# Half of projection tile 0 between modulation tiles 2 and 3, and the first norm in two halves of channels

## The chip, the cores and the metric

The kernel runs on one core of a Trainium2 chip as one launch. The metric is device time in microseconds (us), lower is better. TensorE (PE), VectorE (DVE), ScalarE (ACT), GpSimd (POOL) and SyncE (SP) run their own instruction streams side by side and meet at semaphores. Loads and stores are DMA transfers; nearly all of them are issued by SP, in one queue.

## The reference

One decoder step with one layer (DEPTH = 1), for a prompt of 256 tokens and 8 sequences of 8 sample tokens, together 320 tokens of 1024 channels. What lies around the change:

```python
def _layer(x, c, pos, attend, retain, g_mix, g_ffn, w_ada, b_ada, w_in, ...):
    mod = (jnp.einsum('bd,de->be', jax.nn.silu(c), w_ada) + b_ada)[:, None, :]
    sh1, sc1, gt1, sh2, sc2, gt2 = jnp.split(mod, 6, axis=-1)
    h = _rmsnorm(x, g_mix) * (1.0 + sc1) + sh1
    z = jnp.einsum('bsd,de->bse', h, w_in)
    ...   # rotary, sparse attention, retention, merge, output projection: x
    h2 = _rmsnorm(x, g_ffn) * (1.0 + sc2) + sh2
    x = x + gt2 * _moe(h2, ...)        # top-4 of 32 experts
    return x, (k, v, ik, r_state)
```

The modulation `c` is one row for the prompt and one for each of the 8 sample sequences: 9 rows. All arithmetic is float32.

## The kernel before

**Stages.** First come the statistics of x and the first modulation (sc1 and sh1). Then z is projected in 13 column tiles (`ZT`), with indexer, attention and retention work placed between the tiles. Then come the branch merge and the output projection, the second norm and the router, and at last a loop over 32 experts whose weights (12 MB each) stream through a ring of six chunks. The expert loop asks for a chunk when the chunk before it in that place was used (`chunk_used`).

**The head.** x lies transposed in `actT` (called `hT`: 8 chunks of 128 channels, 320 tokens). ACT squares it (L613), PE sums the squares over channels with a matrix of ones (L871, PSUM bank 4), DVE scales the variance (L1586), ACT takes the root (L615), and DVE refines it (L1588 to L1592) and multiplies all of `hT` by it in one instruction (L1593).

**Modulation tiles.** Four tiles of `w_ada`, 512 columns and 2 MB each, are numbered 0 to 3: scale and shift of channels 0 to 511 (tiles 0, 1), scale and shift of channels 512 to 1023 (tiles 2, 3). For each, PE makes eight products of the nine rows with a weight chunk into 32 partitions (L887, 32x512) and adds one to `tile_done`; ACT copies the bank to `partA` (L618, `part_done`); PE turns the nine rows into columns with four products of nine columns each (`modulation_columns`, L878, `tab_done`); DVE adds the bias and, for a scale tile, the norm gain (L1570, L1572). When both tiles of a half are there, DVE's `modulated(half)` (L1578, L1581 four times, L1583) scales and shifts four chunks of `hT` and raises `h_done`. Tile i lies in PSUM bank i. On PE tile i+1 stands before the columns of tile i.

**Projection tile 0.** `prompt_steps` (L921, L922) makes two products of 128 tokens by up to 512 columns at each of the eight chunks, into banks 0 and 1; `sample_steps` (L934, L935) makes two products of 64 tokens by half of the columns, into bank 2. Steps 0 to 3 need `h_done` 1, steps 4 to 7 `h_done` 2.

**Order.** Everything is written out by hand: each engine executes its stream in program order. SP issues cT, pages, x, constants, columns, then the four `w_ada` tiles, then projection tile 0 (`wz[0]`, 2 MB, in a place of its own), then `wz[1]` after the second modulation tile is done (it takes that tile's place) and `wz[2]`, then the indexer's cached keys (32 of 32 KB), then `wz[3]` once `sample_steps(1)` is done. The buffers before:

```python
beside = [z[:, 5448:9544], ring[:, S0 + 10820:S0 + 14916], ring[:, S0 + 5332:S0 + 9428]]
wm = wt + [x.rearrange("p (k n) -> p k n", k=KT) for x in beside[0:2]]
```

`beside[2]` is the home of `wz[0]`.

Of the kernel before, what the change touches and what calls it, by code (L numbers as in the profile page):

```python
# [16 lines left out]
ALU = mybir.AluOpType  # L17
ACT = mybir.ActivationFunctionType
AX = mybir.AxisListType

P = 128
D = 1024
KT = D // P
SEQ = 256
DB, DS = 8, 8
# [8 lines left out]
NTOK = SEQ + NS  # L34
BANK = 512
# [109 lines left out]
def kern(nc, a):  # L145
    with ExitStack() as ctx:
# [24 lines left out]
        def bank(b, n=1):  # L171
            return ps[:, b * BANK:(b + n) * BANK]
# [3 lines left out]
        hT = actT[:, :].rearrange("p (k n) -> p k n", k=KT)  # L176
        cT3 = cT[:, :].rearrange("p (k n) -> p k n", k=KT)
# [3 lines left out]
        wm = wt + [x.rearrange("p (k n) -> p k n", k=KT) for x in beside[0:2]]  # L181
# [4 lines left out]
        partA = scr(0, 2048)  # L186
        sqT = scr(2048, KT * NTOK).rearrange("p (k n) -> p k n", k=KT)
        var_t, root_t, err_t = scr(4608, NTOK), scr(4928, NTOK), scr(10500, NTOK)
        a1T, sh1T = (mods[:, 72 * i:72 * i + 72].rearrange("p (k c) -> p k c", k=KT) for i in range(2))
        badaT, gmixT = cols[:, 0:6 * KT], cols[:, 6 * KT:7 * KT]  # L190
        junk = scr(9500, 256)
        ident = const("ident")
# [87 lines left out]
        w_here = [sem("w_here0"), sem("w_here1")]  # L280
# [3 lines left out]
        tile_done = sem("tile_done")  # L284
        part_done, tab_done = sem("part_done"), sem("tab_done")
# [24 lines left out]
        st_out, side_here = [sem("st_out0"), sem("st_out1")], [sem(f"side_here{i}") for i in range(3)]  # L310
# [29 lines left out]
        def in_tile(name, s):  # L340

            return a[name][s].rearrange("p (k n) -> p k n", k=KT)
# [10 lines left out]
        def _(sp):  # L353
# [4 lines left out]
            sp.dma_start(cst[:, :], a["const"]).then_inc(g_here, 16)  # L358
            sp.dma_start(cols[:, :], a["cols"]).then_inc(g_here, 16)
            sp.dma_start(prow[:, :], a["page_rows"]).then_inc(pr_here, 16)  # L360
            for i in range(4):
                s = (2, 0, 3, 1)[i]
                sp.dma_start(wm[i], in_tile("w_ada", s)).then_inc(w_here[i] if i < 2 else side_here[i - 2], 16)

            def load_z_tiles(first, last):
                for i in range(first, last):
                    c0, w = ZT[i]
                    if i:
                        sp.wait_ge(tile_done, i + 3 if i >= 3 else 3 - i)
                    sp.dma_start(wz[i], a["w_in"][:, KT * c0:KT * (c0 + w)].rearrange("p (k n) -> p k n", k=KT)).then_inc(w_here[i % 2] if i else side_here[2], 16)  # L370

            def load_tile(n, src, dst=None):

# [16 lines left out]
                        sp.dma_start(ikT[b // 2][64 * j:64 * j + 64, n * PAGE:(n + 1) * PAGE],  # L390
                                     a["cache_ikT"][bass.ds(page, 1)].rearrange("a d s -> (a d) s")).then_inc(keys_here[b // 2], 16)

            load_z_tiles(0, 3)
            sp.wait_ge(pr_here, 32)
            load_index_keys(0, 4)
            load_z_tiles(3, 4)
# [211 lines left out]
        def _(act):  # L608
# [6 lines left out]
            nc.scalar.activation(root_t, var_t, ACT.Sqrt).then_inc(rstd_done, 1)  # L615
            for i in range(4):
                act.wait_ge(tile_done, i + 1)
                nc.scalar.activation(partA[:, i * BANK:(i + 1) * BANK], bank(i), ACT.Copy).then_inc(part_done, 1)  # L618

            gate = [ACT.Copy] * 7 + [ACT.Silu] * 2 + [ACT.Sigmoid] * 4  # L620

# [242 lines left out]
        def _(pe):  # L864
# [4 lines left out]
            for k in range(KT):  # L869
                pe.wait_ge(ss_done, 1 + k // 4)  # L870
                last = nc.tensor.matmul(bank(4)[:, 0:NTOK], const("ones"), sqT[:, k, :], start=k == 0, stop=k == KT - 1)  # L871
            last.then_inc(sq_sum, 1)

            def modulation_columns(i):

                pe.wait_ge(part_done, i + 1)
                for c in range(4):
                    last = nc.tensor.matmul(bank(i)[:, (1 + DB) * c:(1 + DB) * (c + 1)],  # L878
                                            partA[:, i * BANK + c * P:i * BANK + (c + 1) * P], const("selT"),
                                            start=True, stop=True)  # L880
                last.then_inc(tab_done, 1)

            for i in range(4):
                pe.wait_ge(w_here[i] if i < 2 else side_here[i - 2], 16)
                for k in range(KT):
                    g = k % 4
                    last = nc.tensor.matmul(bank(i)[32 * g:32 * g + 32, :], cT3[:, k, :], wm[i][:, k, :],  # L887
                                            start=k < 4, stop=k >= 4)
                last.then_inc(tile_done, 1)
                if i:  # L890
                    modulation_columns(i - 1)
            modulation_columns(3)

            def project(wtile, b, w, x=hT, kt=KT, done=tile_done):

# [12 lines left out]
            def prompt_steps(i, k0, k1):  # L908

                w = ZT[i][1]  # L910
                if k0 == 0:
                    if i:
                        pe.wait_ge(*tile_here(i + 4))
                        pe.wait_ge(zp_out, i)
                    else:
                        pe.wait_ge(side_here[2], 16)
                for k in range(k0, k1):
                    if i == 0 and k % 4 == 0:
                        pe.wait_ge(h_done, 1 + k // 4)
                    se = dict(start=k == 0, stop=k == KT - 1)  # L920
                    nc.tensor.matmul(bank(0)[:, 0:w], hT[:, k, 0:P], wz[i][:, k, 0:w], **se)  # L921
                    last = nc.tensor.matmul(bank(1)[:, 0:w], hT[:, k, P:2 * P], wz[i][:, k, 0:w], **se)  # L922
                if k1 == KT:
                    last.then_inc(zp_done, 1)

            def sample_steps(i):

                w = ZT[i][1]
                h = w // 2
                if i:  # L930
                    pe.wait_ge(z_done, i)
                for k in range(KT):
                    se = dict(start=k == 0, stop=k == KT - 1)
                    nc.tensor.matmul(bank(2)[0:NS, 0:h], hT[:, k, 2 * P:NTOK], wz[i][:, k, 0:h], **se)  # L934
                    last = nc.tensor.matmul(bank(2)[NS:P, 0:h], hT[:, k, 2 * P:NTOK], wz[i][:, k, h:w], **se)  # L935
                last.then_inc(tile_done, 1)

            def key_and_index_query_transposes():

# [65 lines left out]
                    nc.tensor.matmul(bank(5 + k)[0:NS], sel, rel_s[:, k * BANK:(k + 1) * BANK], **se)  # L1005
                nc.tensor.matmul(bank(7)[0:NS, NS:NS + DS], sel, rel_s[:, PAST:KEYS], **se).then_inc(ssel_done, 1)

            for i in range(2):
                prompt_steps(i, 0, KT)
                sample_steps(i)  # L1010
            prompt_steps(2, 0, 4)
            key_and_index_query_transposes()
            prompt_steps(2, 4, KT)
# [21 lines left out]
            for t in range(3):  # L1035
                n = TOK[t]
                last = nc.tensor.transpose(bank(6)[:, t * P:t * P + n], z3[0:n, t, CK:CV], ident[0:n, 0:n])
# [144 lines left out]
            for t in range(3):  # L1182
                n = TOK[t]
                for i in range(2):
# [5 lines left out]
                    for k in range(4):  # L1190
                        last = nc.tensor.transpose(bank(b)[:, at + k * n:at + (k + 1) * n],
                                                   h2[0:n, t, (4 * i + k) * P:(4 * i + k + 1) * P], ident[0:n, 0:n])
# [138 lines left out]
            for i in range(6):  # L1331
# [3 lines left out]
                for k in range(2):  # L1335
                    last = nc.tensor.matmul(bank((0, 6)[i % 2] + k)[0:n, :], sel, partB[2 * (i // 2) + k], start=True, stop=True)  # L1336
# [13 lines left out]
            for t in range(3):  # L1350
                n = TOK[t]
                for k in range(KT):
                    last = nc.tensor.matmul(bank(5)[0:n, t * NE:(t + 1) * NE], hT[:, k, t * P:t * P + n], wr[:, k, :],  # L1353
                                            start=k == 0, stop=k == KT - 1)
# [170 lines left out]
        def _(dve):  # L1525
            steps = [0]

            def step(ins):

                steps[0] += 1  # L1530
                ins.then_inc(dve_step, 1)
                dve.wait_ge(dve_step, steps[0])
# [29 lines left out]
            def modulation_columns(i):  # L1562

                half = i // 2
                chunks = slice(4 * half, 4 * half + 4)
                dst = (a1T, sh1T)[i % 2][:, chunks, :]
                src = bank(i)[:, 0:4 * (1 + DB)].rearrange("p (k c) -> p k c", k=4)
                at = KT * (1 - i % 2) + 4 * half
                dve.wait_ge(tab_done, i + 1)
                step(nc.vector.tensor_tensor(dst, src, badaT[:, at:at + 4].unsqueeze(2).broadcast_to([P, 4, 1 + DB]), ALU.add))  # L1570
                if i % 2 == 0:
                    step(nc.vector.tensor_tensor(dst, dst, gmixT[:, chunks].unsqueeze(2).broadcast_to([P, 4, 1 + DB]), ALU.mult))  # L1572

            def modulated(half):

                s = hT[:, 4 * half:4 * half + 4, SEQ:NTOK].rearrange("p k (b t) -> p k b t", t=DS)
                a_s, sh_s = (m[:, 4 * half:4 * half + 4, 1:1 + DB].unsqueeze(3).broadcast_to([P, 4, DB, DS]) for m in (a1T, sh1T))
                nc.vector.tensor_tensor(s, s, a_s, ALU.mult).then_inc(dve_step, 1)  # L1578
                steps[0] += 1
                for k in range(4 * half, 4 * half + 4):  # L1580
                    last = nc.vector.tensor_scalar(hT[:, k, 0:SEQ], hT[:, k, 0:SEQ], a1T[:, k, 0:1], sh1T[:, k, 0:1], ALU.mult, ALU.add)  # L1581
                dve.wait_ge(dve_step, steps[0])
                nc.vector.tensor_tensor(s, s, sh_s, ALU.add).then_inc(h_done, 1)  # L1583
# [6 lines left out]
            step(nc.vector.tensor_tensor(err_t, err_t, var_t, ALU.mult))  # L1590
            step(nc.vector.tensor_scalar(err_t, err_t, -0.5, 1.5, ALU.mult, ALU.add))
            step(nc.vector.tensor_tensor(root_t, root_t, err_t, ALU.mult))  # L1592
            step(nc.vector.tensor_tensor(hT, hT, root_t.unsqueeze(1).broadcast_to([P, KT, NTOK]), ALU.mult))  # L1593
            modulation_columns(0)
            modulation_columns(1)
            modulated(0)
            modulation_columns(2)
            modulation_columns(3)
            modulated(1)
# [594 lines left out]
```

## Time and profile before

| | us |
|---|---|
| time, median of 3 runs | 1488.99 (1488.91 to 1489.72) |
| the profiled execution's own time | 1483.06 |
| its span, first to last instruction | 1481.2 |
| PE busy | 1395.7 (94%) |
| DVE busy | 454.2 (31%) |
| ACT busy | 220.1 (15%) |
| mean granted PE clock | 0.98 of full speed |

The profiled execution took 1.9 us more than its span, and 5.9 us less than the median of the runs. Times in the rows are those of the profiled execution, from its first instruction on. A float32 product shows as two records on PE, so that eight products of one line are x16. A row of the timeline gives start, duration, engine, line, operation, output and inputs, count, and in brackets how long the engine had been idle before and who released it. The granted clock is 1.00 at 2.4 GHz and 0.50 at 1.2 GHz.

### The profile page before, as it was taken

Reading aid. Unit: us, or ns where it says so; the run is one execution under the profiler, and the core shown is the slowest. Engines: PE = TensorE matmul, PEld = TensorE weight load, DVE = VectorE, ACT = ScalarE, POOL = GpSimd, SP = SyncE. Lnnn points to the kernel's source line nnn. Section 1 sums busy time; section 2 is a strip of 40 time slices with the busy share of each in tenths; the row PEclk is TensorE's granted clock in tenths of the full one; section 3 lists DMA queues with packets and bytes.
Section 4 is the critical chain, followed back from the end, with each engine's and each line's share of the span. In section 5 each row is a group of like instructions: output and inputs, shape, how many; then the busy total and the mean of one; then the engine's idle time right before and its main releaser. Section 6 shows DMA issues by size and latency. Waiting matters only on the chain.

```text
span 1481.2 us, 16979 instructions
## 1 busy us (share of the span) xinstructions
PE 1395.7 (94%) x6475; PEld 567.1 (38%) x6475; DVE 454.2 (31%) x981; ACT 220.1 (15%) x400; POOL 72.2 (5%) x63
## 2 busy tenths in 40 slices
PE   6999999999899599999999999999999999999984
PEld 3544556555434433333333333333333333333321
DVE  5133895753211431221131122113211211121124
ACT  2111222121010211111111111101101111111011
POOL 1002501140000200000000000000000000000000
PEclk8999999999999599999999999999999999999997
DMA  9423254259656179999999999999999999999991
GB/s 393 132 80 142 90 150 144 93 152 359 239 234 263 62 320 428 427 429 427 430 428 429 427 429 428 429 428 429 428 429 428 428 428 428 429 428 429 428 427 54
DMA packets 61664, 488.21 MB, mean 330 GB/s; under 512 B 8266, under 2 KB 30090, under 8 KB 32818
## 3 DMA queue, kind: packets, MB, share of 16 engines
q1 hardware_dynamic: 59314, 482.88, 79.2%
q0 software_dynamic: 1152, 4.19, 0.8%
q8 instruction: 28, 0.46, 0.1%
q10 hardware_dynamic: 1152, 0.52, 0.1%
q14 instruction: 18, 0.15, 0.0%
HBM read 483.46 MB, written 4.08 MB: 329 GB/s over the span
## 4 chain that ended last, share of the span: by engine, by line
DMA 36%; PE 34%; DVE 2%; ACT 1%; issue 1%; POOL 0%; POOLq 0%; DVEq 0%; SPq 0%; ACTq 0%
DMA ring<-in_w_gate_up 36%; PE ps L1452 16%; PE ps L1493 5%; PE ps L1399 2%; PE ps L900 2%; PE ps L901 2%; PE ps L1430 1%; PE ps L904 1%; PE ps L1336 1%; PE ps L1445 1%; PE ps L1353 1%; PE ps L1360 0%; PE ps L1475 0%; PE ps L1407 0%; PE ps L1434 0%
## 5 line engine op out<-in xcount | busy, mean ns | idle before, releaser
L1452 PE MATMUL ps<-ring,z 128*64 128x512 f32 x2048 | 451.3, 595 | 21.1 <-DMA ring<-in_w_gate_up 21.1
L1452 PEld LDWEIGHTS ps<-ring,z 128*64 128x64 f32 x2048 | 142.2, 137 | 327.9 <-issue 277.7
L1493 PE MATMUL ps<-ring,z 128*64 128x512 f32 x1024 | 226.0, 594 | 0.0
L2024 DVE TENSOR_SCALAR actT<-ps 128x512 f32<-128x512 f32 x32 | 22.1, 692 | 648.0 <-PE ps L1452 648.0
L1493 PEld LDWEIGHTS ps<-ring,z 128*64 128x64 f32 x1024 | 72.0, 137 | 149.4 <-issue 145.1
L921 PE MATMUL ps<-ring,actT 128*128 128x512 f32 (+1 forms) x208 | 105.2, 587 | 0.2 <-DMA ring<-in_w_in 0.2
L922 PE MATMUL ps<-ring,actT 128*128 128x512 f32 (+1 forms) x208 | 103.8, 580 | 0.0
L1399 PE MATMUL ps<-z,actT 128*64 128x512 f32 x384 | 88.6, 596 | 1.3 <-DVE actT L1976 1.3
L1430 PE MATMUL ps<-z,aT 128*128 128x512 f32 x128 | 66.2, 619 | 1.7 <-ACT z L833 1.2
L1997 DVE TENSOR_TENSOR z<-z,ps 128x512 f32<-128x512 f32 x64 | 44.0, 688 | 61.3 <-PE ps L1430 61.3
L821 ACT ACTIVATE actT<-actT 128x512 f32<-128x512 f32 x32 | 20.1, 627 | 259.7 <-DVE actT L2024 259.7
L922 PEld LDWEIGHTS ps<-ring,actT 128*128 128x128 f32 x208 | 39.5, 190 | 47.3 <-issue 45.9
L832 ACT ACTIVATE z<-ps 64x512 f32<-64x512 f32 x32 | 18.9, 590 | 247.3 <-PE ps L1493 247.3
L921 PEld LDWEIGHTS ps<-ring,actT 128*128 128x128 f32 x208 | 38.0, 190 | 41.8 <-issue 39.8
L935 PE MATMUL ps<-ring,actT 128*64 128x256 f32 (+1 forms) x208 | 46.5, 376 | 0.0
L934 PE MATMUL ps<-ring,actT 128*64 128x256 f32 (+1 forms) x208 | 46.4, 376 | 0.0
L1673 DVE MAX8 st<-ring 64x8 f32<-64x1032 f32 (+2 forms) x48 | 45.0, 937 | 1.4
L1399 PEld LDWEIGHTS ps<-z,actT 128*64 128x64 f32 x384 | 26.2, 137 | 48.1 <-issue 45.7
L1674 DVE MATCH_REPLACE8 ring<-st,ring 64x1032 f32<-64x1032 f32 (+2 forms) x48 | 44.2, 920 | 0.0
L814 ACT ACTIVATE aT<-ps 128x320 f32<-128x320 f32 x16 | 7.0, 438 | 225.7 <-PE ps L1415 225.7
L1445 PE MATMUL ps<-actT 32*64 32x512 f32 x256 | 34.8, 612 | 0.8 <-ACT z L810 0.8
L1430 PEld LDWEIGHTS ps<-z,aT 128*128 128x128 f32 x128 | 20.6, 190 | 35.4 <-issue 31.5
(323 smaller groups left out, 1210.7 us busy)
## 6 DMA issues: line engine op xcount, KB each, us to landing
ring<-in_w_gate_up SPq DMA_DIRECT2D x128, 2048.0 KB, 23.1
ring<-in_w_down SPq DMA_DIRECT2D x64, 2048.0 KB, 20.6
ring<-in_w_in SPq DMA_DIRECT2D x12, 2048.0 KB, 7.8
ring<-in_w_ada SPq DMA_DIRECT2D x11, 2048.0 KB, 10.2
ring<-in_w_out SPq DMA_DIRECT2D x2, 2048.0 KB, 10.7
z<-in_cache_kT SPq DMA_DIRECT2D x40, 64.0 KB, 1.8
z<-in_w_ada SPq DMA_DIRECT2D x1, 2048.0 KB, 19.0
z<-in_cache_ikT SPq DMA_DIRECT2D x64, 32.0 KB, 2.1
```

Of the source, the lines that this page charges most:

```text
L921: nc.tensor.matmul(bank(0)[:, 0:w], hT[:, k, 0:P], wz[i][:, k, 0:w], **se)
L922: last = nc.tensor.matmul(bank(1)[:, 0:w], hT[:, k, P:2 * P], wz[i][:, k, 0:w], **se)
L934: nc.tensor.matmul(bank(2)[0:NS, 0:h], hT[:, k, 2 * P:NTOK], wz[i][:, k, 0:h], **se)
L935: last = nc.tensor.matmul(bank(2)[NS:P, 0:h], hT[:, k, 2 * P:NTOK], wz[i][:, k, h:w], **se)
L1399: last = nc.tensor.matmul(bank(3)[64 * i:64 * i + 64, :], S[:, t, :], h2[:, t, i * BANK:(i + 1) * BANK], start=t == 0, stop=t == 2)
L1430: nc.tensor.matmul(bank(b), SgT[:, t * P:(t + 1) * P], ysb[buf][:, half * BANK:(half + 1) * BANK], start=True, stop=True).then_inc(cmb_mm, 1)
L1445: nc.tensor.matmul(bank(q // 2)[64 * (q % 2):64 * (q % 2) + 64, :], ebuf[32 * q:32 * q + 32], bgu[32 * q:32 * q + 32], start=True, stop=False)
L1452: done = nc.tensor.matmul(bank(q // 2)[64 * (q % 2):64 * (q % 2) + 64, :], lhs, ring3[k // 2][:, (k % 2) * 2048 + q * BANK:(k % 2) * 2048 ...
L1493: done = nc.tensor.matmul(bank(2)[64 * q:64 * q + 64, :], lhs, ring3[4 + k // 4][:, (k % 4) * D + q * BANK:(k % 4) * D + (q + 1) * BANK], ...
L1673: step(nc.vector.max(m8, v))
L1674: step(nc.vector.match_replace(v, m8, v, TAKEN))
L1997: nc.vector.tensor_tensor(v, v, bank(b), ALU.add).then_inc(acc_done, 1)
```

## The change

SP issues projection tile 0 third of the five 2 MB loads and not fifth: `w_ada` tiles 0 and 1, `wz[0]`, `w_ada` tiles 2 and 3. PE does modulation tiles 0 and 1, both their columns, then steps 0 to 3 of the prompt part of projection tile 0, modulation tile 2, steps 0 to 3 of its sample part, columns 2, modulation tile 3, columns 3, and then steps 4 to 7 of both parts. Modulation tiles 2 and 3 lie in banks 5 and 6, since banks 0 to 2 now hold open sums. DVE multiplies `hT` by the root in two halves; the second stands behind `modulated(0)`. The number of products, transfers and bytes is the same; DVE has one instruction more.

```diff
+        mod_bank = (0, 1, 5, 6)
...
-            for i in range(4):
-                s = (2, 0, 3, 1)[i]
-                sp.dma_start(wm[i], in_tile("w_ada", s)).then_inc(w_here[i] if i < 2 else side_here[i - 2], 16)
+            def load_first_modulation(first, last):
+                for i in range(first, last):
+                    sp.dma_start(wm[i], in_tile("w_ada", (2, 0, 3, 1)[i])).then_inc(w_here[i] if i < 2 else side_here[i - 2], 16)
...
+            load_first_modulation(0, 2)
+            load_z_tiles(0, 1)
+            load_first_modulation(2, 4)
...
-            load_z_tiles(0, 3)
+            load_z_tiles(1, 3)
...
-            for i in range(4):
+            def first_modulation(i):
                 pe.wait_ge(w_here[i] if i < 2 else side_here[i - 2], 16)
...
                 last.then_inc(tile_done, 1)
-                if i:
-                    modulation_columns(i - 1)
-            modulation_columns(3)
+
+            first_modulation(0)
+            first_modulation(1)
+            modulation_columns(0)
+            modulation_columns(1)
...
-            for i in range(2):
-                prompt_steps(i, 0, KT)
-                sample_steps(i)
+            prompt_steps(0, 0, 4)
+            first_modulation(2)
+            sample_steps(0, 0, 4)
+            modulation_columns(2)
+            first_modulation(3)
+            modulation_columns(3)
+            prompt_steps(0, 4, KT)
+            sample_steps(0, 4, KT)
+            prompt_steps(1, 0, KT)
+            sample_steps(1)
...
-            step(nc.vector.tensor_tensor(hT, hT, root_t.unsqueeze(1).broadcast_to([P, KT, NTOK]), ALU.mult))
+
+            def normed(half):
+                h = hT[:, 4 * half:4 * half + 4, :]
+                step(nc.vector.tensor_tensor(h, h, root_t.unsqueeze(1).broadcast_to([P, 4, NTOK]), ALU.mult))
+
+            normed(0)
             modulation_columns(0)
             modulation_columns(1)
             modulated(0)
+            normed(1)
             modulation_columns(2)
             modulation_columns(3)
             modulated(1)
```

The PE stream before, from the sum of squares to the first sample product of projection tile 0. L887 is a modulation tile, L878 its columns, L921 and L922 the prompt steps, L934 and L935 the sample steps:

```order
L871 MATMUL ps<-ring,cst 128x320 x8
L887 MATMUL ps<-ring,cT 32x512 x16
L878 MATMUL ps<-cst,ring 128x9 x4
L887 MATMUL ps<-z,cT 32x512 x8
L878 MATMUL ps<-cst,ring 128x9 x4
L887 MATMUL ps<-ring,cT 32x512 x8
L878 MATMUL ps<-cst,ring 128x9 x8
L921 MATMUL ps<-ring,actT 128x512
L922 MATMUL ps<-ring,actT 128x512
...
L934 MATMUL ps<-ring,actT 64x256
```

The same stretch of PE after the change (L892 is the modulation tile, L883 the columns, L928 and L929 the prompt steps, L941 and L942 the sample steps; each pair of steps stands there four times before the next kind):

```order
L876 MATMUL ps<-ring,cst 128x320 x8
L892 MATMUL ps<-ring,cT 32x512 x16
L883 MATMUL ps<-cst,ring 128x9 x8
L928 MATMUL ps<-ring,actT 128x512
...
L892 MATMUL ps<-z,cT 32x512 x8
L941 MATMUL ps<-ring,actT 64x256
...
L883 MATMUL ps<-cst,ring 128x9 x4
L892 MATMUL ps<-ring,cT 32x512 x8
L883 MATMUL ps<-cst,ring 128x9 x4
L928 MATMUL ps<-ring,actT 128x512
```

Columns 1 no longer stand behind tile 2, and columns 3 are now followed by steps that need them. The DVE stream before, from the norm to the second `modulated`:

```order
L1593 TENSOR_TENSOR actT<-actT,ring 128x2560
L1570 TENSOR_TENSOR mods<-ps,cols 128x36
L1572 TENSOR_TENSOR mods<-mods,cols 128x36
L1570 TENSOR_TENSOR mods<-ps,cols 128x36
L1578 TENSOR_TENSOR actT<-actT,mods 128x4x64
L1581 TENSOR_SCALAR actT<-actT,mods 128x256 x4
L1583 TENSOR_TENSOR actT<-actT,mods 128x4x64
L1570 TENSOR_TENSOR mods<-ps,cols 128x36
```

And after, where L1611 is the norm, L1585 and L1587 the columns, L1593 to L1598 `modulated`:

```order
L1611 TENSOR_TENSOR actT<-actT,ring 128x1280
L1585 TENSOR_TENSOR mods<-ps,cols 128x36
L1587 TENSOR_TENSOR mods<-mods,cols 128x36
L1585 TENSOR_TENSOR mods<-ps,cols 128x36
L1593 TENSOR_TENSOR actT<-actT,mods 128x4x64
L1596 TENSOR_SCALAR actT<-actT,mods 128x256 x4
L1598 TENSOR_TENSOR actT<-actT,mods 128x4x64
L1611 TENSOR_TENSOR actT<-actT,ring 128x1280
L1585 TENSOR_TENSOR mods<-ps,cols 128x36
```

The norm of the second half has moved behind the first `modulated`. On SP the load of `wz[0]` has moved ahead of two `w_ada` loads.

## Rows read from the trace of the kernel before

**Rows 1.** The page: the span, and PE's granted clock in 40 slices.

```profile
span 1481.2 us, 16979 instructions
...
PEclk8999999999999599999999999999999999999997
```

**Rows 2.** The chain that ended last, in time: start us, us, what.

```profile
824.75 25.49 DMA ring<-in_w_gate_up
850.29 3.68 PE ps L1452 x16
```

**Rows 3.** Stretches: length, then busy us (count) of each engine, granted clock, DMA share, GB/s.

```profile
0.00:35.03 35.03, 22.17 (x113) 10.85 (x113) 16.88 (x24) 8.27 (x10) 3.74 (x13) 0.85 0.94 390
35.03:52.56 17.53, 17.53 (x64) 8.20 (x64) 3.11 (x9) 1.08 (x2) 0.00 (x0) 1.00 0.57 179
```

**Rows 4.** Timeline of PE in the head: start, us, engine, line, what.

```profile
18.80 1.92 PE L887 MATMUL ps<-ring,cT 128*32 128x512 f32 x16 [1.53 <-DMA ring<-in_w_ada]
...
20.66 1.06 PE L878 MATMUL ps<-cst,ring 128*128 128x9 f32 x8
23.70 3.64 PE L887 MATMUL ps<-z,cT 128*32 128x512 f32 x16 [1.98 <-DMA z<-in_w_ada]
27.27 1.88 PE L878 MATMUL ps<-cst,ring 128*128 128x9 f32 x8
29.08 3.64 PE L887 MATMUL ps<-ring,cT 128*32 128x512 f32 x16
32.65 2.17 PE L878 MATMUL ps<-cst,ring 128*128 128x9 f32 x16
35.03 1.12 PE L921 MATMUL ps<-ring,actT 128*128 128x512 f32 x2 [0.21 <-DMA ring<-in_w_in]
...
48.96 0.43 PE L934 MATMUL ps<-ring,actT 128*64 128x256 f32 x1
...
52.56 0.82 PE L921 MATMUL ps<-ring,actT 128*128 128x328 f32 x2
```

**Rows 5.** The four loads of line 363, issued from 3.7 to 5.2 us.

```profile
DMA to landing us min/median/max: 10.2/16.8/23.4
```

**Rows 6.** Timeline of DVE in the head.

```profile
20.16 0.49 DVE L1592 TENSOR_TENSOR ring<-ring 128x320 f32<-128x320 f32 x1
20.68 2.82 DVE L1593 TENSOR_TENSOR actT<-actT,ring 128x2560 f32<-128x2560 f32 x1
...
29.26 0.20 DVE L1570 TENSOR_TENSOR mods<-ps,cols 128x36 f32<-128x36 f32 x1 [5.29 <-PE ps L878]
...
31.12 0.41 DVE L1583 TENSOR_TENSOR actT<-actT,mods 128x256 f32<-128x256 f32 x1
...
34.92 0.20 DVE L1570 TENSOR_TENSOR mods<-ps,cols 128x36 f32<-128x36 f32 x1 [0.54 <-PE ps L878]
...
36.79 0.42 DVE L1583 TENSOR_TENSOR actT<-actT,mods 128x256 f32<-128x256 f32 x1
```

**Rows 7.** Timeline of ACT in the head.

```profile
20.79 0.60 ACT L618 ACTIVATE ring<-ps 128x512 f32<-128x512 f32 x1 [2.86 <-PE ps L887]
```

**Rows 8.** Stretches with PE's granted clock: the head, and one later.

```profile
22.75:23.00 0.25, 0.00 (x0) 0.00 (x0) 0.25 (x1) 0.00 (x0) 0.00 (x0) 0.77 1.09 459
...
33.00:33.25 0.25, 0.25 (x4) 0.25 (x3) 0.00 (x0) 0.25 (x1) 0.00 (x0) 0.75 1.09 462
```

**Rows 9.** One later stretch, PE alone: length, busy us (count), granted clock, DMA share, GB/s.

```profile
429.06:432.48 3.42, 1.92 (x16) 1.00 0.41 101
```

**Rows 10.** The router: the timeline of PE, and two stretches with the granted clock.

```profile
512.84 6.26 PE L1360 MATMUL ps<-z,cst 128*128 128x512 f32 x8
...
514.40:517.81 3.41, 3.41 (x5) 0.86 (x4) 1.43 (x10) 1.50 (x4) 0.00 (x0) 0.50 1.03 379
517.81:521.22 3.41, 3.41 (x21) 2.22 (x19) 0.00 (x0) 1.07 (x2) 0.00 (x0) 1.00 1.01 428
```

**Rows 11.** Timeline of SP's queue behind the first loads.

```profile
22.61 39.95 SPq L390 DMA_DIRECT2D z<-in_cache_ikT  x32
64.08 0.34 SPq L370 DMA_DIRECT2D ring<-in_w_in  x1
```

More of the change, by code:

```diff
@@ L617, in _ @@
                 act.wait_ge(tile_done, i + 1)
-                nc.scalar.activation(partA[:, i * BANK:(i + 1) * BANK], bank(i), ACT.Copy).then_inc(part_done, 1)
+                nc.scalar.activation(partA[:, i * BANK:(i + 1) * BANK], bank(mod_bank[i]), ACT.Copy).then_inc(part_done, 1)
             gate = [ACT.Copy] * 7 + [ACT.Silu] * 2 + [ACT.Sigmoid] * 4
@@ L877, in modulation_columns @@
                 for c in range(4):
-                    last = nc.tensor.matmul(bank(i)[:, (1 + DB) * c:(1 + DB) * (c + 1)],
+                    last = nc.tensor.matmul(bank(mod_bank[i])[:, (1 + DB) * c:(1 + DB) * (c + 1)],
                                             partA[:, i * BANK + c * P:i * BANK + (c + 1) * P], const("selT"),
@@ L886, in _ @@
                     g = k % 4
-                    last = nc.tensor.matmul(bank(i)[32 * g:32 * g + 32, :], cT3[:, k, :], wm[i][:, k, :],
+                    last = nc.tensor.matmul(bank(mod_bank[i])[32 * g:32 * g + 32, :], cT3[:, k, :], wm[i][:, k, :],
                                             start=k < 4, stop=k >= 4)
                 last.then_inc(tile_done, 1)
-                if i:
-                    modulation_columns(i - 1)
-            modulation_columns(3)
+            first_modulation(0)
+            first_modulation(1)
+            modulation_columns(0)
+            modulation_columns(1)
             def project(wtile, b, w, x=hT, kt=KT, done=tile_done):
@@ L924, in prompt_steps, with sample_steps @@
                     last.then_inc(zp_done, 1)
-            def sample_steps(i):
+            def sample_steps(i, k0=0, k1=KT):
                 w = ZT[i][1]
@@ L931, in sample_steps @@
                     pe.wait_ge(z_done, i)
-                for k in range(KT):
+                for k in range(k0, k1):
                     se = dict(start=k == 0, stop=k == KT - 1)
@@ L935, in sample_steps @@
                     last = nc.tensor.matmul(bank(2)[NS:P, 0:h], hT[:, k, 2 * P:NTOK], wz[i][:, k, h:w], **se)
-                last.then_inc(tile_done, 1)
+                if k1 == KT:
+                    last.then_inc(tile_done, 1)
             def key_and_index_query_transposes():
@@ L1566, in modulation_columns @@
                 dst = (a1T, sh1T)[i % 2][:, chunks, :]
-                src = bank(i)[:, 0:4 * (1 + DB)].rearrange("p (k c) -> p k c", k=4)
+                src = bank(mod_bank[i])[:, 0:4 * (1 + DB)].rearrange("p (k c) -> p k c", k=4)
                 at = KT * (1 - i % 2) + 4 * half
```

## The prediction

> **What bounds the kernel now.** I read the page first, then the chain of waits, then stretches of the head, and last its timeline, engine by engine.
>
> The end is set by weight traffic: from 824.75 us on the chain alternates between a load of expert weights of 25.49 us and 3.68 us of PE [rows 2]. That stream begins when the first expert's products release the first chunk, so a microsecond won or lost before the experts moves the end by a microsecond. Before the experts PE is the engine that the others follow.
>
> In the head there are two bounds in turn. Up to 35.03 us it is the loads: DMA is 94% busy, and PE 22.17 of 35.03 us [rows 3]. PE waits 1.53 us for the second modulation tile, 1.98 us for the third, and 0.21 us for projection tile 0, the fifth 2 MB load [rows 4]. From 35.03 to 52.56 us PE is busy all the time at full clock: this is projection tile 0 whole [rows 3]. The end of the head is thus 35.03 + 17.53 = 52.56 us, and I compare the two kernels there.
>
> PE's clock matters. Over the span of 1481.2 us it is at 9 or more tenths but for the first slice (8), the fourteenth (5) and the last [rows 1]. In the head it fell to 0.50 in the row 22.75:23.00, where its share 0.77 puts the fall some 0.14 us in, at 22.9 us; it rose again at about 33.1 us [rows 8]. Modulation tile 1 takes 1.92 us at 1.00, tiles 2 and 3 take 3.64 us each at 0.50 [rows 4]. In the kernel before this costs nothing: tiles 2 and 3 finish in time for the fifth load anyway. That cover is what the change touches, because it puts projection steps, which are on the path, into this stretch.
>
> **The loads.** The same five 2 MB loads in another order. The third lands at 23.70 us [rows 4], the fourth at 5.2 + 23.4 = 28.6 us [rows 5], the fifth just before 35.03 us. Now these are projection tile 0, modulation tile 2 and modulation tile 3. wz[1] waits for the second modulation tile as before, and SP's later issues do not move: the 32 key loads run to 62.56 us, and the next projection load went out at 64.08 us behind PE [rows 11]. A head up to 1.5 us shorter passes SP without a wait, a longer one costs nothing there.
>
> **The first half of x.** The norm of 320 columns takes 0.49 us, that of 2560 takes 2.82 us [rows 6]; on the line between them 1280 columns take 1.49 us. So the first half is done at 20.68 + 1.49 = 22.2 us, not 23.5. It gains little, as the second columns come later: columns 0 end on PE at 21.72 us, columns 1 take 1.06 us more [rows 4] and end at 22.8 us (ACT's copy for them was done at 21.39 us [rows 7]). From there to the end of `modulated(0)` it is 0.1 us and then what rows show from 29.26 to 31.53 us, 2.27 us [rows 6]. The first half is ready at 25.15 us, and PE starts its steps at 25.2 us. The extra norm instruction (0.16 us fixed, 1.49 in all) stands behind this, while PE runs steps: nothing.
>
> **PE at full clock.** Eight steps take 48.96 - 35.03 = 13.93 us for the prompt and 52.56 - 48.96 = 3.60 us for the samples [rows 4]. Halves are 6.95 and 1.80 us. A modulation tile occupies PE for 1.85 us, columns for 1.0 us. Chain from 25.2 us: 6.95 (steps) + 1.85 (tile 2, landed at 28.6) + 1.80 (sample steps, which cover ACT's copy) + 1.0 (columns 2) + 1.85 (tile 3, landed by 35.0; PE comes to it at 36.8 or later) gives 38.65 us.
>
> **The new wait.** Before, columns 3 and `modulated(1)` ran under the first four steps: DVE was done at 37.21 us and steps 4 to 7 came at about 42.0 us. Now nothing lies between them and steps 4 to 7. The tail is: ACT's copy, 0.07 + 0.60 us [rows 7], columns 0.05 + 1.06 us [rows 4], DVE 0.10 us and 34.92 to 37.21 us, 2.29 us [rows 6], and 0.05 us to PE: 4.2 us. PE does only 1.06 us of nine-column products in it. Behind this wait stand all of PE's remaining products, and ACT, DVE and SP wait for these. PE resumes at 42.85 us and is through at 42.85 + 6.95 + 1.80 = 51.6 us. **At full clock throughout the head is 52.56 - 51.6 = 1.0 us shorter.**
>
> **The clock.** Two waits of about four microseconds are now in front of projection steps: 20.7 to 25.2 us and 38.65 to 42.85 us, each with little but nine-column products in it. The first exists before (20.7 to 23.7 us), and the clock fell in it. Against a second fall speaks a stretch with PE busy 1.92 of 3.42 us at an unbroken 1.00 [rows 9], but its idle time is 1.5 us, not over 3. I take both falls. How long it then stays down: in the head it rose 4.0 us after dense products had begun at 29.08 us; near the router dense products began at 512.84 us and it rose at 517.81 us, 5.0 us later [rows 10]. The products that ran before 29.08 us, with columns between them, did not raise it. I take 4.0 us each, because steps of 128x512 follow each other without a gap, as tile 3's did: at half clock 4.0 us do the work of 2.0, so each costs 2.0 us (2.5 us by the router's row). Bounds: nothing, if it does not fall; 3 us, if it rises a microsecond later than near the router, since nothing shows that five is the longest.
>
> Sum: -1.0 + 2.0 + 2.0 = **+3.0 us**, 2.5 to 5 us by the rows. The profiled execution would take 1483.06 + 3.0 = 1486.1 us. The runs' median lies 5.9 us above it; if the fall and the rise came otherwise in those runs, the head before may already pay for it. I take off 0.2 us for this and forecast 1488.99 + 2.8 = **1491.8 us**.
>
> The Trainium skill, "TensorE: Matmul & The Clock Gate", section "HAM oscillation — how this bites in real kernels", tells of kernels whose bursts of products are shorter than the waits between them and start at half clock each time. That speaks against this change, since it cuts one unbroken stretch of 17.5 us in two with a wait before each. By the rule the time is the forecast's, without it that of the first rival.
>
> **The rivals.**
> *Clock stays up.* PE has steps, a tile and columns in the stretch that was slow, and the clock holds in both waits. The sum is -1.0 us: 1488.0 us. If the timed runs before lost a microsecond or two at half clock in projection tile 0, it is 1486. For it: rows 9, and the short waits. Against it: the fall at 22.9 us came with PE only 1.2 us idle, and the first wait is now longer.
> *One fall only.* The first costs 2.0 us, the second wait passes or falls so late that it costs little: -1.0 + 2.0 = +1.0 us, 1490.0 us.
> *Slower beyond measurement error.* The same two falls, but the clock comes back late. It decides from 4.0 us of cost together on: at 2.5 us and 3 us it is -1.0 + 5.5 = +4.5 us, 1493.5 us. For it: the router's 5.0 us. A fall in the first wait that begins only while steps run (from 25.2 us) would do the same.
> *The loads don't come in the issue order.* Were wz[0] to land with its old delay behind the tiles, its first steps would start at 28.6 us and not 25.2: +3.4 us more on PE's chain beside the forecast's +2.8, 1495.2 us. Against it: loads landed in the order of issue before, 4.9 us apart [rows 4, 5].
>
> **How the numbers follow.** Two falls as forecast 0.42, late return 0.20, one fall 0.20, clock stays up 0.14, loads 0.04. An effect of 0.2% is 3.0 us, about what a measurement of this kernel can tell from no change. The forecast lies 0.2 us inside it, so a quarter of its chance goes to slower: 0.10 + 0.20 + 0.04 = 0.34 slower. Of clock stays up 0.08 goes to faster, where runs before had paid more, with 0.02 of the rest: 0.10. Same is 0.56. The range takes in clock stays up with a little gain, and late return with its bounds: 1487.2 to 1494.8 us, leaving out the loads and the outer parts of the two.
>
> **What would show it.** Right: PE's first projection step at about 25.2 us and steps 4 to 7 at about 45 us (42.85 and the first fall's 2.0); a wait of about 3 us between columns 3 and them, ended by DVE's second `modulated`; granted clock 0.50 around 25 to 29 us and again in the second wait and for 4 us of steps after it; `sample_steps(0)` over at about 55.5 us. Wrong: clock 1.00 all the way from 30 us on, PE in projection tile 1 by 52 us, or a wait for DMA before the first step. A difference between the kernels' spans that is not the difference at the end of projection tile 0 would show that the way from head to end is not one to one.

## The result and the profile after

| | before | after |
|---|---|---|
| median, 20 runs each | 1484.93 us (1482.28 to 1489.72) | 1489.15 us (1485.85 to 1491.84) |
| after over before | | 1.0025, 95% interval 1.0016 to 1.0034 |
| span of the profiled execution | 1481.2 us | 1487.6 us |
| projection tile 0 over at | 52.56 us | 56.93 us |

The change makes the kernel slower by 3.7 us (1484.93 x 0.0025; 2.4 to 5.0 by the interval). The three runs shown first of the kernel before lay high: over 20 runs its median is 4 us lower. The forecast's 1491.8 us was built on those three, so the forecast is best held against the difference of the two kernels.

PE in the head of the changed kernel; it answers to [rows 4]. Columns: start, us, engine, line, what, and in brackets the idle time before with its releaser.

```profile
18.87 1.92 PE L892 MATMUL ps<-ring,cT 128*32 128x512 f32 x16 [1.42 <-DMA ring<-in_w_ada]
20.72 1.95 PE L883 MATMUL ps<-cst,ring 128*128 128x9 f32 x16
25.27 2.05 PE L928 MATMUL ps<-ring,actT 128*128 128x512 f32 x2 [2.59 <-DVE actT L1598]
27.11 1.91 PE L929 MATMUL ps<-ring,actT 128*128 128x512 f32 x2
28.81 1.63 PE L928 MATMUL ps<-ring,actT 128*128 128x512 f32 x2
30.28 1.02 PE L929 MATMUL ps<-ring,actT 128*128 128x512 f32 x2
...
34.66 1.92 PE L892 MATMUL ps<-z,cT 128*32 128x512 f32 x16
...
38.40 1.06 PE L883 MATMUL ps<-cst,ring 128*128 128x9 f32 x8
39.39 1.92 PE L892 MATMUL ps<-ring,cT 128*32 128x512 f32 x16
42.03 1.06 PE L883 MATMUL ps<-cst,ring 128*128 128x9 f32 x8 [0.72 <-ACT ring L623]
45.53 2.08 PE L928 MATMUL ps<-ring,actT 128*128 128x512 f32 x2 [2.44 <-DVE actT L1598]
47.40 1.92 PE L929 MATMUL ps<-ring,actT 128*128 128x512 f32 x2
49.11 1.72 PE L928 MATMUL ps<-ring,actT 128*128 128x512 f32 x2
50.67 1.02 PE L929 MATMUL ps<-ring,actT 128*128 128x512 f32 x2
...
56.93 0.82 PE L928 MATMUL ps<-ring,actT 128*128 128x328 f32 x2
```

Both groups of steps begin behind a wait for DVE's `modulated` (L1598), 2.59 and 2.44 us, and both begin slow: the first two rows take 1.9 to 2.1 us each, the third 1.63 and 1.72 us, and all behind them 1.02 us. In finer stretches the granted clock fell at 23.2 us and rose at 30.0 us, fell at 43.7 us and rose at 50.5 us, 6.8 us below full speed each time. The stretches of the changed kernel with the granted clock (length, busy us and count of PE, PEld, DVE, ACT and POOL, then granted clock, DMA share, GB/s) show the same; compare [rows 8]:

```profile
23.00:30.20 7.20, 4.93 (x6) 2.19 (x7) 3.49 (x8) 0.00 (x0) 0.00 (x0) 0.53 1.00 426
30.20:43.60 13.40, 12.17 (x75) 5.54 (x73) 0.76 (x4) 1.19 (x2) 0.00 (x0) 1.00 1.03 362
43.60:50.50 6.90, 4.97 (x6) 2.19 (x7) 2.85 (x8) 0.00 (x0) 0.00 (x0) 0.51 0.13 30
50.50:57.00 6.50, 6.50 (x28) 2.84 (x26) 0.00 (x0) 1.08 (x2) 0.00 (x0) 1.00 0.10 28
```

The span grew by 6.4 us, the head by 4.37. The first expert's products start at 532.6 us, not 528.5: 4.1 us of it arrive there. The other 2.3 us are near the end. Before and after, from the chain that ended last (start us, us, what):

```profile
1412.15 25.49 DMA ring<-in_w_gate_up
1444.99 1.72 PE ps L1430 x4
1446.71 7.04 PE ps L1493 x32
```

```profile
1386.61 26.58 DMA ring<-in_w_gate_up
1449.76 3.08 PE ps L1445 x4
1452.83 7.33 PE ps L1508 x32
```

In the changed kernel's execution one load took 26.58 us and not 25.49, and the clock fell once more near 1450 us: four products took 3.08 us, not 1.72. That is 2.7 us with the 0.3 us behind it; other pieces were a little shorter. The fall at the end is not a part of the change: the changed kernel's other profile (e11) has 1.72 us for the four products, and of the other kernels below e3 and e5 have 3.34 and 3.38 us there, all others 1.72. The median of the runs grew by 4.2 us, near the head's 4.4.

### The profile page after: what moved, and what is told of

It is laid out like the page before. It is cut to its first block, busy times and chain, and to the rows that moved or that the text cites. A ratio compares the mean times of both kernels' runs of the same rounds, so it can differ in the third digit from the quotient of the medians.

```text
span 1487.6 us, 16981 instructions
## 1 busy us (share of the span) xinstructions
PE 1397.7 (94%) x6475; PEld 567.8 (38%) x6475; DVE 454.3 (31%) x982; ACT 220.1 (15%) x400; POOL 72.1 (5%) x63
## 4 chain that ended last, share of the span: by engine, by line
DMA 36%; PE 33%; DVE 2%; ACT 1%; issue 1%; POOL 0%; POOLq 0%; DVEq 0%; SPq 0%; ACTq 0%
DMA ring<-in_w_gate_up 36%; PE ps L1467 15%; PE ps L1508 5%; PE ps L1414 2%; PE ps L907 2%; PE ps L908 2%; PE ps L1445 1%; PE ps L911 1%; PE ps L1351 1%; PE ps L1460 1%; PE ps L1368 1%; PE ps L1375 0%; PE ps L1490 0%; PE ps L1422 0%; PE ps L1449 0%
## 5 line engine op out<-in xcount | busy, mean ns | idle before, releaser
L928 PE MATMUL ps<-ring,actT 128*128 128x512 f32 (+1 forms) x208 | 108.5, 604 | 5.0 <-DVE actT L1598 5.0
L929 PE MATMUL ps<-ring,actT 128*128 128x512 f32 (+1 forms) x208 | 105.5, 589 | 0.0
L929 PEld LDWEIGHTS ps<-ring,actT 128*128 128x128 f32 x208 | 40.4, 194 | 49.1 <-issue 47.8
L928 PEld LDWEIGHTS ps<-ring,actT 128*128 128x128 f32 x208 | 38.9, 195 | 47.3 <-issue 43.1
L942 PE MATMUL ps<-ring,actT 128*64 128x256 f32 (+1 forms) x208 | 46.7, 377 | 0.0
L941 PE MATMUL ps<-ring,actT 128*64 128x256 f32 (+1 forms) x208 | 46.6, 376 | 0.0
```

## The experiments

"Tile 0 over" is the start of the first 128x328 product in the profiled execution, "modulation from" the start of modulation tile 0 on PE, which follows the sums of squares, and "steps from" that of the first projection step. Ratios are to the kernel before, measured beside it on the same chip, with 95% intervals, 11 or 12 runs of each experiment. There are three groups, each on a chip of its own: e1 to e4, e5 to e8, e9 to e11. On the first and third chip all seven profiles show a wait of 3.0 us for ACT between 335 and 350 us where the others show 0.9, so whole spans are compared within a group only.

| kernel | modulation from, us | steps from, us | tile 0 over, us | ratio to before |
|---|---|---|---|---|
| before | 15.34 | 35.03 | 52.56 | |
| changed | 15.52 | 25.27 | 56.93 | 1.0025 (1.0016 to 1.0034) |
| e1 both waits filled | 16.34 | 26.08 | 52.92 | 0.9995 (0.9978 to 1.0012) |
| e2 second filled | 15.91 | 25.65 | 54.84 | 1.0016 (1.0002 to 1.0029) |
| e3 first filled | 16.06 | 25.81 | 54.34 | 1.0008 (0.9992 to 1.0023) |
| e4 norm whole | 16.69 | 27.77 | 59.23 | 1.0041 (1.0026 to 1.0056) |
| e5 real work in the second wait | 16.50 | 26.24 | 53.06 | 0.9993 (0.9979 to 1.0007) |
| e6 before, loads reordered | 15.50 | 37.56 | 55.07 | 1.0009 (0.9998 to 1.0020) |
| e7 before, norm in halves | 15.34 | 34.50 | 54.82 | 0.9999 (0.9988 to 1.0010) |
| e8 before, one wait filled | 16.33 | 34.53 | 53.76 | 1.0001 (0.9989 to 1.0014) |
| e9 e5 with the first wait filled | 15.69 | 25.66 | 49.80 | 0.9966 (0.9950 to 0.9982) |
| e10 before, three waits filled | 16.08 | 34.81 | 52.35 | 1.0001 (0.9986 to 1.0017) |
| e11 the changed kernel again | 16.42 | 26.17 | 58.52 | 1.0034 (1.0017 to 1.0050) |

The first two columns hold something that must be taken off before two heads are compared. In the changed kernel and in e1, e2, e3, e5 and e11 the first steps start 9.74 or 9.75 us behind modulation tile 0, whatever its start; the chain between them is DVE's. Modulation tile 0 itself starts anywhere from 15.34 to 16.69 us. So part of a difference between two such heads is only this start. In the kernel before, the fifth load releases the first steps (34.5 to 35.0 us), and the start does not show.

### Is it the clock: e1, e2, e3

```diff
+            def filler(n):
+                for _ in range(n):
+                    nc.tensor.matmul(bank(7)[:, 0:256], const("ones"), cst[:, 0:256], start=True, stop=True)
...
+            filler(6)                     # e1, e3
             prompt_steps(0, 0, 4)
...
             first_modulation(3)
+            filler(1)                     # e1, e2
             modulation_columns(3)
+            filler(5)                     # e1, e2
             prompt_steps(0, 4, KT)
```

> The changed kernel plus twelve products of ones with constants (128x256, 0.43 us each at full clock) into the unused bank 7: six in front of prompt steps 0 to 3, one between modulation tile 3 and its columns, five behind columns 3. They compute nothing that is used and only keep PE at work in its two waits. Theory 'clock' (the loss is the two falls of PE's clock in the waits, 2 to 2.3 us each): granted clock stays 1.00 through the head, projection tile 0 is over near 52.0 us where the changed kernel has 56.9, and the time is about 4.5 us under the changed kernel, 0 to 1 us under the kernel before. Rival 'tail' (the loss is the work order itself, the uncovered way from columns 3 to the second half of x, and the clock only shifts it): projection tile 0 is over at 56 us or later, time as the changed kernel or a little more. Mixed case: the fall in the first wait comes all the same, since nine-column products remain in it; then about 2 us under the changed kernel.

> The changed kernel with the fill products in the second wait alone (one before columns 3, five behind). Theory 'clock': the first slow stretch stays (25 to 30 us), the second (43.7 to 50.5 us) goes; projection tile 0 over at 54.6 us, 2.3 us before the changed kernel, time +2 us against the kernel before. Rival 'tail': 56.9 us or later.

> The changed kernel with the six fill products in the first wait alone. Theory 'clock': if the fall is avoided, steps 0 to 3 run at full clock from 25.3 us and are over at 32.2 and not 34.6 us, modulation tile 3 then starts at 36.8 us; the second wait still brings a fall, unless it falls together with other idle time differently; projection tile 0 over at about 54.5 us. Rival 'tail': no change, 56.9 us.

Stretches of e1, of e2 (two rows) and of e3, with the granted clock:

```profile
18.00:52.90 34.90, 33.31 (x172) 17.25 (x168) 12.64 (x27) 3.47 (x6) 0.00 (x0) 1.00 0.78 297
```

```profile
23.00:30.50 7.50, 4.96 (x8) 2.21 (x8) 3.84 (x9) 0.00 (x0) 0.00 (x0) 0.54 1.01 428
30.50:54.80 24.30, 24.03 (x119) 11.60 (x117) 3.61 (x11) 2.28 (x4) 0.00 (x0) 1.00 0.61 212
```

```profile
44.75:48.25 3.50, 3.50 (x6) 1.46 (x5) 0.10 (x1) 0.00 (x0) 0.00 (x0) 0.52 0.12 31
```

With both waits filled the clock stays at 1.00 throughout, the steps still wait for DVE (0.71 and 0.18 us behind the fill), and tile 0 is over 4.0 us sooner than in the changed kernel. The second fill alone gives 2.1 us, the first alone 2.6 us; in e3 the second fall came later and shorter, 3.5 us. The three executions also began modulation tile 0 later than the changed kernel's, by 0.8, 0.4 and 0.5 us. Counted from that start, the fills give 4.8 us (both), 2.5 us (second) and 3.1 us (first, with the shorter second fall). The products compute nothing, so what they give back is the clock's cost: 4.8 us, which is more than the whole 4.4 us by which the changed kernel's head is longer. "Tail" alone is refuted. With the clock held, tile 0 ends at 52.9 us against 52.6 before; with modulation tile 0 starting where the changed kernel's did, it would be 52.1 us (an estimate, 52.92 - 0.82). So the order by itself gains about 0.5 us where I had worked out 1.0, and only where the sums of squares end early. In time e1 stands at -0.7 us against before (2.5 us either way), where the changed kernel stood at +3.7 us against before, on another chip.

### The parts: e4, e6, e7

e4 is the changed kernel with `normed(0)` made the whole norm and `normed(1)` taken out; e7 is the kernel before with `normed(0)` in place of the norm and `normed(1)` behind `modulated(0)`. e6 is the kernel before with only this:

```diff
-            for i in range(4):
-                s = (2, 0, 3, 1)[i]
-                sp.dma_start(wm[i], in_tile("w_ada", s)).then_inc(w_here[i] if i < 2 else side_here[i - 2], 16)
+            load_first_modulation(0, 2)
+            load_z_tiles(0, 1)
+            load_first_modulation(2, 4)
```

> The changed kernel with the norm of x in one instruction as before. The first half of x then waits for the whole norm: 20.86 + 2.85 = 23.7 us, then 0.43 + 0.23 + 2.05 us: ready at 26.4 us, not 25.1. By the theory that PE's chain sets the end, projection tile 0 ends 1.0 to 1.3 us later than in the changed kernel (some of it lies at half clock, where a later start costs less): about 58.0 us. If the order of loads and not DVE released the first steps it would change nothing.

> The kernel before with only the order of the loads changed (projection tile 0 third, modulation tiles 2 and 3 fourth and fifth); PE and DVE as before. Modulation tile 2 starts at 28.6 and tile 3 at 35.0 us; then 1.85 us of tile 3 (3.6 at half clock), ACT's copy 0.7 us, columns 1 us. Steps 0 to 3 need only the first half of x and begin behind columns 3, at 38.7 us at full clock and 42 us at half, so projection tile 0 is over at 56.2 to 60 us: +3.7 to +7 us. It shows what the load order costs that the placed steps have to earn back. If loads do not follow the issue order, the change is smaller.

> The kernel before with only the norm in two halves. The first half of x is ready at about 31.6 us either way since columns 1 come at 29.2 us, and PE waits for its load until 35.03 us: no change, 0 within 0.5 us in the head.

PE in e4 and in e6:

```profile
27.77 2.05 PE L928 MATMUL ps<-ring,actT 128*128 128x512 f32 x2 [4.99 <-DVE actT L1598]
```

```profile
29.00 3.64 PE L891 MATMUL ps<-z,cT 128*32 128x512 f32 x16 [6.87 <-DMA z<-in_w_ada]
32.57 1.35 PE L882 MATMUL ps<-cst,ring 128*128 128x9 f32 x8
33.90 1.92 PE L891 MATMUL ps<-ring,cT 128*32 128x512 f32 x16
35.75 1.95 PE L882 MATMUL ps<-cst,ring 128*128 128x9 f32 x16
37.56 1.10 PE L925 MATMUL ps<-ring,actT 128*128 128x512 f32 x2
```

e4: without the halves the first steps start at 27.77 us, 2.5 us later than in the changed kernel and 1.6 us later than in its repetition e11 (26.17 us), and tile 0 is over 2.3 or 0.7 us later. Counted from modulation tile 0 the steps start 11.08 us behind it, not 9.74: the norm in halves is worth 1.34 us at the first steps, as costed (23.5 - 22.2 = 1.3 us). DVE, not a load, releases the first steps. e7: in the kernel before the halves change nothing in time.

e6: with the load order alone tile 0 is over 2.5 us later than in the profile of before, but only 0.3 and 1.3 us later than in e7 and e8, which ran on the same chip and lost time to slow steps. In time it stands at +1.3 us (-0.3 to +3.0). All this is less than the 3.7 to 7 us expected. The idle time before modulation tile 2 is there, 6.87 us, but tile 3 runs at 33.90 us without waiting: the last `w_ada` load, issued at 6.2 us, took 27.6 us and landed at 33.8 us. Over all profiles a `w_ada` load in the fifth place landed at 33.5 to 34.7 us, projection tile 0 in the fifth place at 34.5 to 35.0 us. And the clock came back in time for tile 3 and all steps.

e7's execution shows something else: its clock fell at about 33.3 us, while PE waited for the load of projection tile 0, and the steps began at half clock:

```profile
34.50:40.75 6.25, 6.25 (x8) 2.71 (x9) 1.09 (x3) 0.00 (x0) 0.00 (x0) 0.55 0.98 411
```

PE's work and the loads up to there are those of the kernel before, whose own profile has 1.00 in this place [rows 3]. So the head of before need not always be over at 52.6 us; only one profile of it exists.

### Can the kernel before gain: e8, e10

Fill products (as in e1) in the kernel before: e8 has five before modulation tile 2, e10 also four before tile 3 and four before projection tile 0.

> The kernel before with five fill products (128x256) in its wait for modulation tile 2. 'Clock' expects the fall at 22.9 us to be avoided, tiles 2 and 3 to take 1.92 us each, and yet the end of projection tile 0 at 52.5 us to stay, since the fifth load sets 35.03 us: no change in time. If the kernel before pays for its own slow stretch in executions other than the one profiled, its median falls by 1 to 2 us.

> The kernel before with unused products (128x256) in all three waits of its head: five before modulation tile 2, four before tile 3, four before projection tile 0. The profile of e7, whose work is that of the kernel before, had steps at half clock from 34.5 us on and tile 0 over at 54.8 us. If such executions are in the median of before, filling all waits brings projection tile 0 to 52.5 us each time and the median 1 to 1.5 us down. The fill before tile 0 may delay it by up to 0.9 us where the load was there already. Otherwise no change.

In e10 the clock is 1.00 all through the head and tile 0 is over at 52.35 us, yet the time is that of the kernel before (1.0001). In e8 the fall came later, at 28.5 us, and tile 3 took 3.45 us after a wait of 1.81 us for its load. A second fall came at 35.3 us, 0.8 us into the steps, and held for 3.4 us, so that tile 0 was over at 53.76 us. Neither shows a gain in time, and the 1 to 1.5 us that e10 might have brought is not there. That executions like e7's weigh in the median of before is thus not shown.

### A version that beats both: e5, e9, e11

```diff
             prompt_steps(0, 0, 4)
             first_modulation(2)
-            sample_steps(0, 0, 4)
-            modulation_columns(2)
             first_modulation(3)
+            modulation_columns(2)
             modulation_columns(3)
+            sample_steps(0, 0, 4)
             prompt_steps(0, 4, KT)
```

e9 has `filler(6)` in front of `prompt_steps(0, 0, 4)` besides.

> The changed kernel with PE's order inside the changed stretch altered: prompt steps 0 to 3, modulation tile 2, modulation tile 3, columns 2, columns 3, then sample steps 0 to 3 and only then prompt steps 4 to 7. Columns 2 cover ACT's copy of tile 3, and real work of 1.8 us lies in the second wait. Both theories expect the wait in front of steps 4 to 7 to shrink from 2.6 us to about 0.6 us and PE to reach them near 43.0 us, not 45.5. 'Clock' expects also that the second fall is avoided: projection tile 0 over near 51.8 us, 0.7 us before the kernel before; if it falls all the same, 53.9 us. 'Tail' expects 2.5 us off the changed kernel, 54.4 us.

> The kernel of e5 (sample steps 0 to 3 in the second wait) plus six unused products of 128x256 in the first wait. In e1 those products kept the clock at 1.00, and steps 0 to 3 began at 26.1 us; from there 6.95 + 1.85 + 1.85 + 1.9 + 1.8 us of work and 0.6 us of wait reach steps 4 to 7 at about 41.0 us, and projection tile 0 is over at 49.8 to 50.5 us. Theory 'clock': 2.3 us under the kernel before in the head, and 3 us or more under its median, which also holds executions with a slow stretch in projection tile 0: 1482 to 1483 where before has 1486. Rival: the gain of the head does not reach the end (the expert weights' stream starts when it did): no change against before.

> The changed kernel as it is, on the same chip as e9 and e10, for a direct comparison: 1.0025 of the kernel before, projection tile 0 over at 56 to 58 us.

PE in e5, then in e9 (its line 898 is the fill, and 1603 is the end of `modulated`, as 1598 in e5):

```profile
26.24 2.04 PE L928 MATMUL ps<-ring,actT 128*128 128x512 f32 x2 [3.41 <-DVE actT L1598]
...
44.12 1.13 PE L928 MATMUL ps<-ring,actT 128*128 128x512 f32 x2 [0.57 <-DVE actT L1598]
```

```profile
22.98 2.84 PE L898 MATMUL ps<-cst 128*128 128x256 f32 x12
25.66 1.10 PE L932 MATMUL ps<-ring,actT 128*128 128x512 f32 x2
...
34.61 1.92 PE L892 MATMUL ps<-ring,cT 128*32 128x512 f32 x16
36.46 1.95 PE L883 MATMUL ps<-cst,ring 128*128 128x9 f32 x16
...
40.86 1.12 PE L932 MATMUL ps<-ring,actT 128*128 128x512 f32 x2 [0.57 <-DVE actT L1603]
...
49.80 0.82 PE L932 MATMUL ps<-ring,actT 128*128 128x328 f32 x2
```

In e5 the wait in front of steps 4 to 7 is 0.57 us and they start at full clock (1.13 us, not 2.08): the second fall is gone, the first is still there. Tile 0 is over at 53.06 us, 3.9 us before the changed kernel (4.9 us counted from modulation tile 0), and the time is that of the kernel before. It was expected near 51.8 us, from steps that start at 25.3 us; they started at 26.24. e11 came out at 58.52 us and 1.0034, a little beyond the 56 to 58 us expected. In e9 both falls are gone and steps 4 to 7 begin at 40.86 us. Against e11 in the same group the head is 58.52 - 49.80 = 8.7 us shorter, the first expert's products start 541.27 - 532.88 = 8.4 us sooner, the span is 8.1 us shorter, and the median 1495.67 - 1486.46 = 9.2 us: the head reaches the end one to one, to about half a microsecond. Of the 8.7 us, 0.7 is the earlier start of modulation tile 0 (15.69 against 16.42 us). Against the kernel before e9 gains 0.34% (0.18 to 0.50%): 5.1 us by the ratio, 4.6 us by the medians, and 2.8 us by the profiles' heads, of which before's is from another chip. It is the one version that is clearly faster than both.

## Why the prediction held, point by point

**The bound and the place.** That PE's chain through the head sets the start of the expert stream, and moves the end one to one, is shown: head +4.37, first expert +4.1, medians +4.2 us; e9 against e11 again.

**The loads.** The order of landing was that of issue. The fifth landed at 5.8 + 27.7 = 33.5 us, not 35.0, which nobody waited for. The rival of a late projection tile 0 fell. Its price of 3.4 us was also too low for what it says: 28.6 us is the landing of the fourth load, and behind both tiles the projection tile would have been the fifth, near 35 us.

**The first half of x.** Forecast 25.15 us, PE from 25.2: measured 25.27, released by DVE. The half norm took 1.49 us, as worked out. That the total came so close is in part luck: the prediction took the start of this chain from one profile as fixed, and in e11 the same kernel's steps began at 26.17 us.

**The two waits.** Forecast 4.2 us for the second between tile 3 and step 4. Measured 45.53 - 41.31 (39.39 + 1.92) = 4.22 us. The wait between columns 3 and the steps was 2.44 us, which is what the terms of the tail give; the "about 3 us" among the signs did not follow from them.

**The clock.** Forecast: two falls, half clock during 4.0 us of steps each, 2.0 us each. Both came. But steps ran slow from 25.27 to 30.0 and from 45.53 to 50.5 us, 4.8 and 5.0 us: 2.4 and 2.5 us. This is the mis-sized term: the router's 5.0 us [rows 10] was the better row, and the head's 4.0 us was taken. Added to the full-clock sum it gives 51.6 + 4.9 = 56.5 us, against 56.93 measured, with 0.2 us for the later start of modulation tile 0 in this execution. The fills measure the same cost in another way: 4.8 us. In the repetition e11 steps ran slow for 5.7 and 5.4 us (26.17 to 31.9, 46.89 to 52.3 us), in e5's first wait for 5.8 us, in e4 for 4.5 and 4.8 us. So no single length holds, and 4.0 us was below all of them; what repeats in the changed kernel is the 6.8 us from fall to rise, in all four falls of its two profiles, and the cost is the part of it in which steps run. The late-return rival had its point of decision at 4.0 us of cost for both falls together and its example at 5.5. With 4.9 us here and 5.6 us in e11 that rival is what happened.

**The sum.** Forecast +2.8 us, just inside 0.2%; measured +3.7 us, just outside. The case I held likeliest had the right mechanism and lost 0.9 us in size. The measured 1489.15 us lies 2.7 us below the forecast's 1491.8 all the same, because the kernel before came out 4 us lower over 20 runs than over three; that it is inside the range says little about the terms. The 1.0 us that I gave to the work order at full clock is not there in e1 (52.92 against 52.56), whose modulation tile 0 started at 16.34 us, not 15.34. The order gains about 0.5 us where this start is early and nothing where it is a microsecond late, because it puts the way from the sums of squares on the path, where the kernel before waited for a load. The deduction of 0.2 us for executions of before with a slow stretch rested on a thing that e7's profile shows to exist, and that e10 does not show in the median.

**Clock stays up; one fall only.** Neither happened in the two profiles of the changed kernel. e1 and e2 show what they would have given.

## What to carry to other kernels

Work that is moved forward into a wait may have covered another wait where it stood. Here steps covered the way from the last columns through DVE to the second half of x, and the change took this cover away. The new wait has to be taken off what the move gains. Before placing work on the path between two waits, read the granted clock there: a slow stretch that cost nothing under a load costs full price once the work in it is on the path. Keep a piece of independent real work for the last wait (e5), and if a wait can't be filled with real work, products that compute nothing can keep the clock (e9).

## What the runs showed of the hardware

The same work does not always meet the same clock. With the order of the kernel before up to the steps, the clock fell once in its own profile, at 22.9 us, and in e7's twice, at 23.1 and 33.3 us, and one stretch of steps ran at 1.00 in one and 0.55 in the other; tile 0 was over at 52.56 and 54.82 us. The changed kernel's head took 56.93 and 58.52 us in two executions on two chips: its first steps began at 25.27 and 26.17 us because the sums of squares ended later. Their end depends on when the pace of their products doubles. In the profile of before their weight loads start 0.53 us apart up to 12.46 us, and the last nine take 2.44 us:

```profile
12.46 2.44 PEld L871 LDWEIGHTS ps<-ring,cst 128*128 128x128 f32 x9 [0.20 <-issue]
```

In e11 they stand 0.53 us apart up to 14.64 us, and only the last five are fast (1.34 us). The rows give a granted clock of 1.00 in this stretch in both profiles, so that the clock is the reason is likely but not shown. A single profile of such a head is good to about a microsecond or two.

A fall does not need a long idle time just before it. At 22.9 us in before PE had been idle for 1.2 us, behind nine-column products; at 35.3 us in e8 it had been in the steps for 0.8 us, behind nine-column products and 0.44 us of idle time.

In all seven profiles from two of the chips (e1 to e4, e9 to e11) PE waited 3.0 us for ACT between 335 and 350 us, and 0.9 us in the six others; ACT itself stood 2.3 us (3.1 us in e11) in the middle of six copies of one line, for a reason that the trace calls remote. This is e10:

```profile
336.29 0.66 ACT L740 ACTIVATE actT<-ps 128x256 f32<-128x256 f32 x2 [2.27 <-remote]
```

What it waited for is open.
